# The up/down seam of a hybrid decoder block's MLP: loads placed ahead of a reload, a rectified block moved, additions that free banks placed ahead of sums and low parts

## The chip, the cores and the metric

One core of a Trainium2 chip runs the whole program. The metric is the device time of one launch in microseconds; the kernel before was timed in three runs, and one more execution was profiled.

## The reference

The reference is one decoder layer on a sequence of 1024 tokens of width 1024: two attention mixers, a gate and an output projection, and then the MLP that this case is about, in float32:

```
h = _rms_norm(x, norm_mlp_g[l])
x = x + jnp.square(jax.nn.relu(h @ w_up[l])) @ w_down[l]
return _rms_norm(x, norm_final_g)
```

`w_up` is 1024 x 4096 and `w_down` 4096 x 1024.

## The kernel before, in words

Both products of the MLP are cut into blocks `n`, 16 for `w_up` (n = 0 to 15; `UP` is 16) and 32 for `w_down` (n = 16 to 47). A block is a 2 x 2 product of halves, made with seven products `P1, P2, P6, P5, P7, P4, P3` and some additions of weight blocks and of hidden blocks instead of eight products. Each operand is split into a high part (a cast, made by ScalarE) and a low part (the remainder, made by VectorE), and three products high x high, high x low, low x high stand for one. One product of an up block is 12 matmuls on 128 x 512, one of a down block is 6.

Every engine runs a list that is written out by hand, and semaphores tie the lists together. Around the seam these names count:

- TensorE: `block_products(n)` gives the order. Block 16 of the list is (16,P1) (15,P7) (14,P3) (16,P6) (15,P4) (16,P2) (16,P5) (15,P3); block 17 is (17,P1) (16,P7) (17,P6) (16,P4) (17,P2) (17,P5) (16,P3); from 18 on it is (n,P1) (n-1,P7) (n-1,P3) (n,P6) (n-1,P4) (n,P2) (n,P5). So (18,P4) is the fifth product of block 19.
- The products add up in PSUM banks that are shared between neighbouring blocks. `copy_s1(n)` (L1986) and `copy_s2(n)` (L1998) on ScalarE copy a bank where the next products add on. `dn_add(n, what)` (L2398, `keep<-keep,ps`) on VectorE adds a finished quarter "11", "12", "21" or "22" of a down block to its place in the eight tiles `kp` of 128 x 1024, and so frees its bank: (n,P4) waits for `dn_add(n, "22")`, (n+2,P1) waits for `dn_add(n, "21")`, `copy_s1(n+1)` for `dn_add(n, "11")` and `copy_s2(n+1)` for `dn_add(n, "12")`.
- The tiles of `kp` hold hidden blocks while the up product runs. Before a `dn_add` of blocks 16 to 19 can add to a tile, the residual has to be brought back: `reload(m)` (L885, `keep<-x_mid`, 512 KB) on SyncE's queue. Blocks 16, 17, 18 and 19 use tiles (0,2), (1,3), (4,6) and (5,7), quarters "11" and "12" the first and "21" and "22" the second.
- `load_form(c, j)` (L857, `dn_raw<-hidden`, 512 KB) loads form `j` of the hidden blocks for group `c` of four down blocks. `dn_hi(c, j)` (L2026) and `dn_lo(c, j)` (L2398, `dn_b<-dn_raw,dn_b`) make its high and low parts. Group 0 serves blocks 16 to 19, group 1 blocks 20 to 23.
- `load_a(u, what)` (L841, 256 KB each) loads four blocks of weights for two down blocks. `sums(u)` (L2398, `a_raw` and `spare`) makes their four sums; `form_hi` (L1976) and `form_lo` (L2567) split them.
- `up_c12(q)`, `up_r12(q)` (L2716), `square_12(q)` finish a quarter of up block q; `t_sums(q)` (L2398, `keep<-keep` x4) makes four sums of its quarters, and `store_t(q)` writes them to memory.

All transfers of this stretch are issued by SyncE, in the order of its list, where a transfer stands behind the waits of those ahead of it. Of the waits in that list one counts below:

```
load_unit(UP + 2)
for j in (P2, P5, P7, P4, P3):
    load_form(1, j)
sp.wait_ge(t_ok, 4 * UP - 1)
sp.wait_ge(u11_out[1], 16 * (UP // 2))
reload(4)
```

`t_ok` reaches that count when the third addition of `t_sums(15)` is done.

Of the kernel before, what the change touches and what calls it, by code (L numbers as in the profile page):

```python
# [134 lines left out]
def last_use(u, j):  # L135

    return PRODUCT[u if u < UP else 2 * u - UP + 1, j]
# [27 lines left out]

def dn_forms(n):

    early = {UP + 2: [(1, P6), (1, P2)], UP + 3: [(1, P5), (1, P7)], UP + 4: [(1, P4), (1, P3)]}
    if n in early:
        return early[n]  # L170
    c, pos = divmod(n - UP, 4)
    c += 1 if pos else 0
    if c < 2 or c > 7:
        return []
    return [(c, j) for j in ((P3,), (P1, P6, P2), (P5,), (P7, P4))[pos]]
# [120 lines left out]
def build(nc, x, g_attn, w_in, b_forget, w_branch, w_out, g_mlp, w_up, w_down, g_final, rope, f_rows, r_rows, m_rows, a_rows, x_mid, hidden, sg, out):  # L296
# [8 lines left out]
    with ExitStack() as ctx:  # L305
# [416 lines left out]
        def _(sp):  # L722
# [120 lines left out]
            def load_form(c, j):  # L843

                if c >= 2:
                    sp.wait_ge(done, PRODUCT[UP + 4 * c - 5, j])
                    sp.wait_ge(b_hi, D_FORM[c - 1, j])
                else:
                    sp.wait_ge(done, PRODUCT[UP - 1, P7 if j == P5 else j])
                    if c == 1:  # L850
                        sp.wait_ge(b_hi, D_FORM[0, j])
                if j in (P1, P3):
                    for i in range(2):
                        sp.wait_ge((u11_out if j == P1 else u22_out)[i], 16 * (c + 1))
                else:
                    sp.wait_ge({P2: u21_out, P6: t2_out, P5: t1_out, P7: t3_out, P4: t4_out}[j], 16 * (2 * c + 2))
                sp.dma_start(dn_raw[j][:, c % 2, 1, :, :],  # L857
                             hidden[2 * c:2 * c + 2, j].rearrange("k p c -> p k c")).then_inc(tile_in[j], 16)
# [23 lines left out]
            def reload(m):  # L882
                for i in range(2):
                    sp.wait_ge(x_out[i], 64)
                sp.dma_start(kp[:, m, :], x_mid[m]).then_inc(x_back[m], 16)  # L885
# [138 lines left out]
            sp.wait_ge(u22_out[0], 16 * (UP // 2))  # L1024
            reload(1)
            load_form(0, P3)
            sp.wait_ge(r12_ok, UP)
            reload(3)

            def load_unit(u):  # L1030
                sp.wait_ge(a_lo, A_FORM[u - 2, 2])
                load_a(u, "a21")
                load_a(u, "a22")
                if u == UP + 2:
                    load_form(1, P1)
                    load_form(1, P6)
                sp.wait_ge(done, last_use(u - 2, P1))
                load_a(u, "a11")
                sp.wait_ge(done, last_use(u - 2, P2))
                load_a(u, "a12")  # L1040
# [541 lines left out]
        def _(act):  # L1582
# [382 lines left out]
            def form_hi(q, b):  # L1965

                if b == 0:
                    act.wait_ge(a_in[q % 4], 64 * (q // 4 + 1 + (NG // 2 if q % 4 < 2 else 0)))
                else:
                    act.wait_ge(a_sum, 4 * NG + 4 * q + (0, 3, 4)[b])  # L1970
                if q >= 2:
                    act.wait_ge(done, last_use(q - 2, (P2, P5, P3)[b]))
                elif q == 1:
                    act.wait_ge(w_used, CH_OUT + (KC - 1 if b == 0 else KC))
                src = third_raw(q) if b == 2 else a_raw_t[q % 2][b]
                act.copy(a_hi_t[q % 2][b][:], src[:]).then_inc(a_hi, 1)  # L1976

            def copy_s1(q):
                act.wait_ge(done, PRODUCT[q, P1])
                if q < 2:  # L1980
                    act.wait_ge(hf_lo, H_FORM["t13", 0])
                elif q <= UP:
                    act.wait_ge(r11_ok, q - 1)
                else:
                    act.wait_ge(c11_ok, q - UP + 2)
                act.copy(s1[q] if q < 2 else bank_b(q), bank_a(q)).then_inc(s1_ok, 1)  # L1986
# [13 lines left out]
            def copy_s3(q):  # L2000
                act.wait_ge(done, PRODUCT[q, P7])
                if q == 0:
                    act.wait_ge(hf_lo, H_FORM["t13", 2])
                else:
                    act.wait_ge(c22_ok, NG + q)
                act.copy(s3, bank_a(q)).then_inc(s3_ok, 1)
# [5 lines left out]
            def square_22(q):  # L2012
                square_hidden(u22[q % 2], r22_ok, q + 1, u22_ok)

            def square_12(q):
                square_hidden(u12, r12_ok, q + 1, u12_ok)
# [7 lines left out]
            def dn_hi(c, j):  # L2024
                act.wait_ge(tile_in[j], 16 * (c + 2))
                act.copy(dn_b[j][:, c % 2, 0, :, :], dn_raw[j][:, c % 2, 1, :, :]).then_inc(b_hi, 1)  # L2026
# [60 lines left out]
                square_11(n)  # L2087
            copy_s1(UP)
            copy_s3(UP - 1)
            square_22(UP - 1)  # L2090
            square_12(UP - 2)
            dn_hi(0, P2)
            form_hi(UP, 2)
            dn_hi(0, P5)
            copy_s2(UP)
            dn_hi(0, P7)
            square_21(UP - 1)
            dn_hi(0, P4)
            copy_s1(UP + 1)
            square_12(UP - 1)  # L2100
            form_hi(UP + 1, 0)
            dn_hi(0, P3)
            form_hi(UP + 1, 1)
            dn_hi(1, P1)
            copy_s2(UP + 1)
            form_hi(UP + 1, 2)

# [43 lines left out]
        def _(dve):  # L2151
# [541 lines left out]
            def up_r22(q):  # L2693
                dve.wait_ge(c22_ok, NG + q + 1)
                dve.scalar_tensor_tensor(out=u22[q % 2], in0=u22[q % 2], scalar=0.0, in1=rstd_r,
                                         op0=ALU.max, op1=ALU.mult).then_inc(r22_ok, 1)
# [11 lines left out]
            def up_c12(q):  # L2708
                dve.wait_ge(done, PRODUCT[q, P3])
                dve.wait_ge(s2_ok, NG + q + 1)  # L2710
                after(dve, t1_out, 16 * q)
                add(u12, bank_c(q), s2[q % 2]).then_inc(c12_ok, 1)
# [89 lines left out]
            dn_lo(0, P6)  # L2802
            up_c22(UP - 1)
            up_r22(UP - 1)
            up_c12(UP - 2)
            up_r12(UP - 2)
            dn_lo(0, P2)
            t_sums(UP - 2, (1, 2))
            dn_lo(0, P5)
            form_lo(UP, 2)  # L2810
            t_sums(UP - 2, (3, 4))
            up_r21(UP - 1)
            dn_lo(0, P7)
            dn_add(UP, "11")
            sums(UP + 1)
            up_c12(UP - 1)
            up_r12(UP - 1)
            dn_lo(0, P4)
            dn_add(UP, "22")
            form_lo(UP + 1, 0)  # L2820
            dn_add(UP, "21")
            dn_lo(0, P3)
            dn_add(UP + 1, "11")
            form_lo(UP + 1, 1)
            dn_add(UP, "12")
            t_sums(UP - 1)
            dn_lo(1, P1)
            dn_add(UP + 1, "22")
            for n in range(UP + 2, NB + 1):
                forms = dn_forms(n)  # L2830
                u = form_of(n) + 1
                more = u < N_FORM and n > UP + 1
                if n >= NB:
                    ends = final_events(n - 1)
                    dn_add(n - 1, "22")
                    dn_last(n - 1, "22")
                    for i in ends[:2]:
                        final_sum(i)
                    dn_add(n - 1, "12")
                    dn_last(n - 1, "12")  # L2840
                    for i in ends[2:]:
                        final_sum(i)
                    dn_add(n - 1, "21")
                elif n % 2 == 0:
                    form_lo(u - 1, 2)
                    if more:
                        sums(u, (1,))
                    if n > UP + 2:
                        dn_add(n - 1, "22")
                    if more:  # L2850
                        sums(u, (2,))
                    dn_add(n - 1, "12")
                    if more:
                        sums(u, (3, 4))
                    dn_add(n - 1, "21")
                    for x in forms:
                        dn_lo(*x)
                    dn_add(n, "11")
                else:
                    for x in forms[:2]:  # L2860
                        dn_lo(*x)
                    dn_add(n - 1, "22")
                    if more:
                        form_lo(u, 0)
                    dn_add(n - 1, "12")
                    if more:
                        form_lo(u, 1)
                    dn_add(n - 1, "21")
                    for x in forms[2:]:
                        dn_lo(*x)  # L2870
                    dn_add(n, "11")
                if NB > n > NB - 4:
                    dn_last(n - 1, "22")
                    dn_last(n - 1, "12")
                for i in final_events(n) if n != NB - 1 else ():
                    final_sum(i)
# [61 lines left out]
```

## Time and profile before

| | |
|---|---|
| median of 3 runs | 1521.97 us (1521.58 to 1523.61) |
| profiled execution | 1520.79 us, of which the span is 1519.0 us |
| TensorE busy | 1489.0 us, 98% of the span |
| VectorE busy | 1089.4 us, 72% |
| ScalarE busy | 793.7 us, 52% |
| granted TensorE clock, mean | 0.997 |

The span runs from the first to the last instruction of the program. The up product begins at about 874 us of it, the first down product at 1172.9 us, and the last down product ends at about 1496 us. A busy share is an average over the whole program; the seam is a stretch of some 50 us of it.

### The profile page before, as it was taken

How to read it: one execution, taken by the hardware profiler on the slowest of the kernel's cores; microseconds unless marked ns; L12 is line 12 of the kernel's file. 1: busy time of each engine (PE TensorE's matmuls, PEld its weight loads, DVE VectorE, ACT ScalarE, POOL GpSimd, SP SyncE). 2: the span in 40 equal slices, each digit the busy share in tenths (PEclk: the TensorE clock that was granted, in tenths of full speed). 3: DMA queues.
4: the chain of work that ended last, by engine and by line, in shares of the span. 5: the costliest groups of instructions: out<-in, count | busy, mean ns of one | idle time of the engine just before them, and what ended most of it. 6: DMA issues, size and time to landing. Idle time of an engine off the chain costs nothing.

```text
span 1519.0 us, 20720 instructions
## 1 busy us (share of the span) xinstructions
PE 1489.0 (98%) x7283; PEld 1235.1 (81%) x7283; DVE 1089.4 (72%) x1745; ACT 793.7 (52%) x1440; POOL 18.6 (1%) x29
## 2 busy tenths in 40 slices
PE   7999999999999999999999999999999899999997
PEld 6888888887888888888888888888888688888886
DVE  5787777756786778543765686667667898888876
ACT  6577766665677775444234553333434544444432
POOL 0000000000000200000000000000000000000001
PEclk9999999999999999999999999999999999999998
DMA  5221111114222014334545434444445964444402
GB/s 194 71 70 29 43 56 43 29 45 101 70 70 71 15 43 127 96 104 149 180 135 140 139 104 164 154 153 152 152 153 178 313 214 152 152 153 152 153 28 111
DMA packets 171061, 176.78 MB, mean 116 GB/s; under 512 B 9576, under 2 KB 129736, under 8 KB 170576
## 3 DMA queue, kind: packets, MB, share of 16 engines
q1 hardware_dynamic: 170960, 175.46, 36.3%
q8 instruction: 60, 0.98, 0.3%
q14 instruction: 41, 0.34, 0.1%
HBM read 129.08 MB, written 46.35 MB: 115 GB/s over the span
## 4 chain that ended last, share of the span: by engine, by line
PE 87%; DVE 6%; ACT 2%; issue 2%; DMA 2%; SPq 1%; DVEq 0%; ACTq 0%
PE ps L1545 37%; PE ps L1204 20%; PE ps L1405 8%; PE ps L1149 4%; PE ps L1436 4%; PE ps L1280 3%; PE ps L1247 3%; PE ps L1259 3%; PE ps L1346 1%; DVE keep L2398 1%; PE ps L1138 1%; PE ps L1173 1%; DVE keep L2293 1%; DVE ps L2271 1%; PE ps L1293 0%
## 5 line engine op out<-in xcount | busy, mean ns | idle before, releaser
L1204 PE MATMUL ps<-hspl,wsp 128*128 128x512 f32 x1536 | 419.5, 407 | 0.4 <-ACT tmp L1634 0.4
L1204 PEld LDWEIGHTS ps<-hspl,wsp 128*128 128x128 f32 x1536 | 265.8, 189 | 43.5 <-ACT tmp L1634 0.6
L1545 PE MATMUL ps<-dn_b,a_hi 128*128 128x512 f32 x896 | 276.4, 390 | 5.7 <-DVE keep L2398 3.5
L1545 PEld LDWEIGHTS ps<-dn_b,a_hi 128*128 128x128 f32 x896 | 167.6, 188 | 43.0 <-issue 7.4
L1545 PE MATMUL ps<-dn_b,a_lo 128*128 128x512 f32 x448 | 174.3, 389 | 0.0
L2398 DVE TENSOR_TENSOR keep<-keep,ps 128x512 f32<-128x512 f32 (+1 forms) x144 | 102.1, 714 | 60.0 <-PE ps L1545 41.0
L1545 PE MATMUL ps<-up_b,a_hi 128*128 128x512 f32 x384 | 118.5, 390 | 0.2 <-DVE up_b L2398 0.2
L2010 ACT ACTIVATE keep<-keep 128x512 f32<-128x512 f32 x64 | 40.5, 633 | 126.6 <-DVE keep L2705 42.0
L1545 PEld LDWEIGHTS ps<-dn_b,a_lo 128*128 128x128 f32 x448 | 84.1, 188 | 17.5
L2567 DVE TENSOR_TENSOR a_lo<-a_raw,a_hi 128x1024 fp32r<-128x1024 f32 (+1 forms) x66 | 81.3, 1234 | 9.5 <-ACT a_hi L1976 9.3
L2293 DVE TENSOR_TENSOR keep<-ps,o_part 64x256 f32<-64x256 f32 x80 | 39.8, 497 | 62.7 <-ACT o_part L1725 61.3
L1545 PEld LDWEIGHTS ps<-up_b,a_hi 128*128 128x128 f32 x384 | 71.9, 188 | 15.6 <-DVE up_b L2398 0.7
L1986 ACT COPY ps<-ps 128x512 f32<-128x512 f32 x46 | 26.3, 571 | 111.4 <-PE ps L1545 109.1
L1545 PE MATMUL ps<-up_t,a_hi 128*128 128x512 f32 x256 | 79.1, 390 | 0.1
L1545 PE MATMUL ps<-up_t4b,a_hi 128*128 128x512 f32 x256 | 78.8, 389 | 0.0
L1710 ACT CAST work<-ps 128x128 fp32r<-128x128 f32 (+3 forms) x144 | 50.8, 365 | 51.1 <-PE ps L1259 50.1
L1259 PE MATMUL ps<-ident,tmp 128*128 128x128 f32 x428 | 73.4, 274 | 2.7 <-ACT tmp L1702 2.4
L1545 PE MATMUL ps<-up_b,a_lo 128*128 128x512 f32 x192 | 74.7, 389 | 0.0
L1280 PEld LDWEIGHTS ps<-work 128*128 128x128 f32 x456 | 68.3, 190 | 6.0 <-issue 0.2
L1259 PEld LDWEIGHTS ps<-ident,tmp 128*128 128x128 f32 x428 | 53.7, 140 | 22.7 <-ACT tmp L1702 8.5
L2398 DVE TENSOR_TENSOR dn_b<-dn_raw,dn_b 128x1024 fp32r<-128x1024 f32 x56 | 67.0, 1219 | 3.9 <-ACT dn_b L2026 3.9
L1976 ACT CAST a_hi<-a_raw 128x1024 fp32r<-128x1024 f32 (+1 forms) x66 | 68.3, 1060 | 2.3 <-DMA a_raw<-in_w_up 2.2
(227 smaller groups left out, 2804.5 us busy)
## 6 DMA issues: line engine op xcount, KB each, us to landing
hidden<-keep SPq DMA_DIRECT2D x112, 256.0 KB, 2.2
dn_raw<-hidden SPq DMA_DIRECT2D x56, 512.0 KB, 6.1
raw<-in_w_in SPq DMA_DIRECT2D x35, 512.0 KB, 3.8
a_raw<-in_w_up SPq DMA_DIRECT2D x36, 256.0 KB, 3.1
sgl<-sg SPq DMA_DIRECT2D x8, 1024.0 KB, 5.0
a_raw<-in_w_down SPq DMA_DIRECT2D x32, 256.0 KB, 3.0
spare<-in_w_down SPq DMA_DIRECT2D x32, 256.0 KB, 3.7
spare<-in_w_up SPq DMA_DIRECT2D x28, 256.0 KB, 3.1
```

What stands on the lines that cost most here:

```text
L1149: ins = pe.matmul(ps[:, cols], w(wp, k), mv(mp, k)[:, cols], start=(k == 0 and n == 0), stop=(k == ks - 1 and n == 2))
L1204: ins = pe.matmul(psp(u, g), wsp[c % 2][:, wp, k * P:(k + 1) * P], hspl[:, mp, k, cols], start=(n == 0), stop=(n == 23), skip_group_check= ...
L1259: ins = pe.transpose(o[:, (k - a) * P:(k - a + 1) * P], probs(G)[:, k * P:(k + 1) * P], ident[:])
L1280: ins = pe.matmul(o[:, cols], v_nat[:, j, 2 * (b % 2):2 * (b % 2) + 2, :].rearrange("p a d -> p (a d)"), moving, start=(part == 0 and (n = ...
L1405: ins = pe.matmul(o, (a_hi_t, a_lo_t)[wp][q % 2][b][:, i, k * P:(k + 1) * P], gate_b(j, mp, k), start=(j in (P1, P5) and k == 0 and m == 0 ...
L1436: ins = pe.matmul(banks[a][:, cols], w_of(c)(wp, k), br_in[:, mp, k, cols], start=(k == ks[0] and n == 0), stop=(k == ks[-1] and n == 2), ...
L1545: ins = pe.matmul(o, a_part(n, j, wp, k), b_block(n, j, mp, k), start=(first and k == 0 and m == 0), stop=(k == ks - 1 and m == 2), skip_g ...
L1710: act.copy(pt_tiles(G, 0, a, b), tr_bank(G, u)[:, 0:(b - a) * P].rearrange("p (j c) -> p j c", c=P)).then_inc(pt_hi, 1)
L1976: act.copy(a_hi_t[q % 2][b][:], src[:]).then_inc(a_hi, 1)
L2293: dve.tensor_tensor(pair_tokens(dst[row:row + 64], t, b // 2), pair_view(o_bank(B)[row:row + 64, :], t), pair_view(o_part[row:row + 64, :] ...
L2398: return dve.tensor_tensor(out, a, b, op)
L2567: dve.tensor_tensor(a_lo_t[q % 2][b][:], src[:], a_hi_t[q % 2][b][:].bitcast(F32), ALU.subtract).then_inc(a_lo, 1)
```

## The change

SyncE's list: `load_form(1, P1)`, the first two weight blocks of unit 18 and `load_form(1, P6)` are issued ahead of the wait for `up_r12(15)` and of `reload(3)`, which stood in front of them. ScalarE's list: `dn_hi(0, ...)` of P2, P5 and P3 each stand ahead of a square or a cast; `square_12(15)` stands behind both casts of unit 17; `dn_hi(1, P1)` moves from in front of `copy_s2(17)` to block 18. VectorE's list: `dn_lo(0, P2)` stands ahead of `up_c12(14)`; `dn_add(16, "22")` ahead of `sums(17)`; `dn_add(16, "12")` and `dn_add(17, "22")` each move ahead; `dn_lo(1, P1)` moves to block 18, and there all sums and low parts stand behind the three additions. TensorE's list does not change.

```
 def dn_forms(n):
-    early = {UP + 2: [(1, P6), (1, P2)], UP + 3: [(1, P5), (1, P7)], UP + 4: [(1, P4), (1, P3)]}
+    early = {UP + 2: [(1, P1), (1, P6), (1, P2)], UP + 3: [(1, P5), (1, P7)], UP + 4: [(1, P4), (1, P3)]}
...
             load_form(0, P3)
-            sp.wait_ge(r12_ok, UP)
-            reload(3)
+            load_form(1, P1)
             def load_unit(u):
                 sp.wait_ge(a_lo, A_FORM[u - 2, 2])
                 load_a(u, "a21")
                 load_a(u, "a22")
                 if u == UP + 2:
-                    load_form(1, P1)
                     load_form(1, P6)
+                    sp.wait_ge(r12_ok, UP)
+                    reload(3)
...
             copy_s3(UP - 1)
+            dn_hi(0, P2)
             square_22(UP - 1)
+            form_hi(UP, 2)
             square_12(UP - 2)
-            dn_hi(0, P2)
-            form_hi(UP, 2)
             dn_hi(0, P5)
...
             copy_s1(UP + 1)
+            dn_hi(0, P3)
+            form_hi(UP + 1, 0)
+            form_hi(UP + 1, 1)
             square_12(UP - 1)
-            form_hi(UP + 1, 0)
-            dn_hi(0, P3)
-            form_hi(UP + 1, 1)
-            dn_hi(1, P1)
             copy_s2(UP + 1)
             form_hi(UP + 1, 2)
...
+            dn_lo(0, P2)
             up_c12(UP - 2)
             up_r12(UP - 2)
-            dn_lo(0, P2)
-            t_sums(UP - 2, (1, 2))
+            t_sums(UP - 2, (1,))
             dn_lo(0, P5)
+            t_sums(UP - 2, (2,))
             form_lo(UP, 2)
             t_sums(UP - 2, (3, 4))
             up_r21(UP - 1)
             dn_lo(0, P7)
             dn_add(UP, "11")
+            dn_lo(0, P4)
+            dn_add(UP, "22")
             sums(UP + 1)
             up_c12(UP - 1)
             up_r12(UP - 1)
-            dn_lo(0, P4)
-            dn_add(UP, "22")
+            dn_lo(0, P3)
+            dn_add(UP, "21")
             form_lo(UP + 1, 0)
-            dn_add(UP, "21")
-            dn_lo(0, P3)
+            dn_add(UP, "12")
             dn_add(UP + 1, "11")
             form_lo(UP + 1, 1)
-            dn_add(UP, "12")
+            dn_add(UP + 1, "22")
             t_sums(UP - 1)
-            dn_lo(1, P1)
-            dn_add(UP + 1, "22")
             for n in range(UP + 2, NB + 1):
...
+                elif n == UP + 2:
+                    form_lo(u - 1, 2)
+                    dn_add(n - 1, "12")
+                    dn_add(n - 1, "21")
+                    dn_add(n, "11")
+                    sums(u)
+                    for x in forms:
+                        dn_lo(*x)
```

In SyncE's list, between the reload of tile 1 and the third weight block of unit 18, the two lists differ as follows (`keep<-x_mid` is a reload: the first row that of tile 1, the moved one that of tile 3; `dn_raw_103`, `97` and `99` are forms P3 of group 0 and P1 and P6 of group 1):

```order
 L885 DMA keep<-x_mid 128x1024
 L857 DMA dn_raw_103<-hidden 128x2x512
-L885 DMA keep<-x_mid 128x1024
-L841 DMA spare_88<-in_w_down 128x2x256 x2
-L857 DMA dn_raw_97<-hidden 128x2x512
-L857 DMA dn_raw_99<-hidden 128x2x512
+L857 DMA dn_raw_97<-hidden 128x2x512
+L841 DMA spare_88<-in_w_down 128x2x256 x2
+L857 DMA dn_raw_99<-hidden 128x2x512
+L885 DMA keep<-x_mid 128x1024
 L841 DMA a_raw_0_82<-in_w_down 128x2x256 x2
 L857 DMA dn_raw_98<-hidden 128x2x512
```

The reload of tile 3 goes behind two forms and two weight blocks. The reload of tile 4, which comes after five more forms, keeps its place.

In VectorE's list of before, this stands from the two sums after `form_lo(17, 2)` to `dn_add(18, "22")` (`keep_51<-keep_51,ps` is a `dn_add`: "12" and "21" of block 17, "11" and "22" of block 18; `a_raw0` and `spare0` are `sums(18)`; `dn_b2`, `1`, `3`, `4` are the low parts of forms P6, P2, P5, P7 of group 1):

```order
L2398 TENSOR_TENSOR spare0_88<-a_raw0_0_82,spare0_88 128x512
L2398 TENSOR_TENSOR keep_51<-keep_51,ps3 128x512
L2398 TENSOR_TENSOR a_raw0_1_83<-a_raw0_1_83,a_raw0_0_82 128x512
L2398 TENSOR_TENSOR spare0_88<-a_raw0_0_82,a_raw0_1_83 128x512
L2398 TENSOR_TENSOR keep_51<-keep_51,ps0 128x512
L2398 TENSOR_TENSOR dn_b2_92<-dn_raw2_99,dn_b2_92 128x1024
L2398 TENSOR_TENSOR dn_b1_91<-dn_raw1_98,dn_b1_91 128x1024
L2398 TENSOR_TENSOR keep_51<-keep_51,ps3 128x512
L2398 TENSOR_TENSOR dn_b3_93<-dn_raw3_100,dn_b3_93 128x1024
L2398 TENSOR_TENSOR dn_b4_94<-dn_raw4_101,dn_b4_94 128x1024
L2398 TENSOR_TENSOR keep_51<-keep_51,ps0 128x512
```

In VectorE's list of the changed kernel, the same stretch from `dn_add(17, "21")` on reads (lines are one less there; `dn_b0` is form P1):

```order
L2397 TENSOR_TENSOR keep_51<-keep_51,ps0 128x512
L2397 TENSOR_TENSOR keep_51<-keep_51,ps3 128x512
L2397 TENSOR_TENSOR a_raw0_1_83<-spare0_88 128x512
L2397 TENSOR_TENSOR spare0_88<-a_raw0_0_82,spare0_88 128x512
L2397 TENSOR_TENSOR a_raw0_1_83<-a_raw0_1_83,a_raw0_0_82 128x512
L2397 TENSOR_TENSOR spare0_88<-a_raw0_0_82,a_raw0_1_83 128x512
L2397 TENSOR_TENSOR dn_b0_90<-dn_raw0_97,dn_b0_90 128x1024
L2397 TENSOR_TENSOR dn_b2_92<-dn_raw2_99,dn_b2_92 128x1024
L2397 TENSOR_TENSOR dn_b1_91<-dn_raw1_98,dn_b1_91 128x1024
L2397 TENSOR_TENSOR dn_b3_93<-dn_raw3_100,dn_b3_93 128x1024
L2397 TENSOR_TENSOR dn_b4_94<-dn_raw4_101,dn_b4_94 128x1024
L2397 TENSOR_TENSOR keep_51<-keep_51,ps0 128x512
```

`dn_add(18, "11")`, the second row, moved from behind two low parts to the front of `sums(18)`; between it and `dn_add(18, "22")`, the last row, there are now four sums and five low parts, where there were two low parts.

## Rows read from the trace of the kernel before

**Rows 1.** Windows: start:end, length, PE, PEld, DVE, ACT, POOL busy, PEclk, DMA, GB/s.

```profile
1190.00:1200.00 10.00, 7.25 (x33) 5.69 (x32) 9.22 (x13) 5.61 (x7) 0.00 (x0) 1.00 0.81 263
1200.00:1210.00 10.00, 9.10 (x41) 7.23 (x40) 9.33 (x12) 5.35 (x6) 0.00 (x0) 1.00 1.04 372
1210.00:1220.00 10.00, 9.93 (x44) 7.78 (x42) 9.93 (x13) 4.96 (x6) 0.00 (x0) 1.00 0.87 315
```

**Rows 2.** TensorE's waits from 1100 to 1496: total us, times, longest.

```profile
PE ps L1545 <- DVE keep L2398: 3.5, 2, 2.8
PE ps L1545 <- issue: 1.3, 2, 0.9
PE ps L1545 <- ACT ps L1998: 0.9, 1, 0.9
```

**Rows 3.** TensorE's timeline at the seam: start, us, instruction, idle before and releaser.

```profile
1184.28 0.70 PE L1545 MATMUL ps<-dn_b,a_hi 128*128 128x512 f32 x2 [0.35 <-issue]
...
1186.84 0.69 PE L1545 MATMUL ps<-dn_b,a_hi 128*128 128x512 f32 x2 [0.94 <-issue]
...
1198.04 0.70 PE L1545 MATMUL ps<-dn_b,a_hi 128*128 128x512 f32 x2 [2.75 <-DVE keep L2398]
...
1202.23 0.61 PE L1545 MATMUL ps<-dn_b,a_hi 128*128 128x512 f32 x2
...
1203.60 0.61 PE L1545 MATMUL ps<-dn_b,a_hi 128*128 128x512 f32 x2
...
1206.02 0.70 PE L1545 MATMUL ps<-dn_b,a_hi 128*128 128x512 f32 x2 [0.90 <-ACT ps L1998]
...
1220.25 0.70 PE L1545 MATMUL ps<-dn_b,a_hi 128*128 128x512 f32 x2
```

**Rows 4.** VectorE's timeline, from the low part of (0, P2) on.

```profile
1182.95 1.23 DVE L2398 TENSOR_TENSOR dn_b<-dn_raw,dn_b 128x1024 fp32r<-128x1024 f32 x1 [1.64 <-ACT dn_b L2026]
...
1204.40 2.71 DVE L2398 TENSOR_TENSOR keep<-keep 128x512 f32<-128x512 f32 x4
...
1208.77 1.75 DVE L2567 TENSOR_TENSOR a_lo<-spare,a_hi 128x1536 fp32r<-128x1536 f32 x1
1210.43 0.68 DVE L2398 TENSOR_TENSOR a_raw<-spare 128x512 f32<-128x512 f32 x1
...
1214.28 2.35 DVE L2398 TENSOR_TENSOR dn_b<-dn_raw,dn_b 128x1024 fp32r<-128x1024 f32 x2
...
1217.15 2.35 DVE L2398 TENSOR_TENSOR dn_b<-dn_raw,dn_b 128x1024 fp32r<-128x1024 f32 x2
1219.42 0.68 DVE L2398 TENSOR_TENSOR keep<-keep,ps 128x512 f32<-128x512 f32 x1
```

**Rows 5.** SyncE's queue: issues of the reloads of tiles 1 and 4.

```profile
1191.62 0.32 SPq L885 DMA_DIRECT2D keep<-x_mid  x1
...
1206.54 0.33 SPq L885 DMA_DIRECT2D keep<-x_mid  x1
```

**Rows 6.** Issue to landing, us: form P2 at 1173.38, reloads at 1191.62, 1196.18, 1206.54, 1215.72.

```profile
dn_raw<-hidden SPq DMA_DIRECT2D x1, 512.0 KB, 5.4
...
keep<-x_mid SPq DMA_DIRECT2D x1, 512.0 KB, 4.0
...
keep<-x_mid SPq DMA_DIRECT2D x1, 512.0 KB, 3.5
...
keep<-x_mid SPq DMA_DIRECT2D x1, 512.0 KB, 8.5
...
keep<-x_mid SPq DMA_DIRECT2D x1, 512.0 KB, 3.4
```

**Rows 7.** ScalarE's timeline: the high part of (1, P1), ahead of `copy_s2(17)`.

```profile
1204.34 1.05 ACT L2026 CAST dn_b<-dn_raw 128x1024 fp32r<-128x1024 f32 x1 [4.69 <-DMA dn_raw<-hidden]
```

**Rows 8.** Windows of the program's tail, columns as in Rows 1.

```profile
1500.00:1505.00 5.00, 3.56 (x27) 3.24 (x28) 4.14 (x7) 0.69 (x2) 0.00 (x0) 0.86 0.00 0
1505.00:1510.00 5.00, 5.00 (x26) 5.00 (x25) 3.30 (x5) 1.44 (x3) 2.36 (x1) 0.50 0.52 210
```

## The prediction

> **What bounds the kernel now.** I read the totals first: TensorE is busy for 98% of the span, so only a stretch where it waits can give time back. The list of its waits from the last up products to the last down product shows that there is little: 5.7 us in all [rows 2]. The timeline puts 4.9 us of it at the seam, in front of (16,P2) at 1184.28, (16,P5) at 1186.84, (16,P4) at 1198.04 and (17,P7) at 1206.02 [rows 3]. The reader should then look at who is late there. The windows show VectorE busy for 9.22, 9.33 and 9.93 us of three stretches of ten, and a DMA share of 0.81 to 1.04 [rows 1]. So from about 1183 to 1220 the seam is bound by VectorE's list, fed by a full queue. At 1220.25 TensorE starts (18,P4), 0.15 us after the end of `dn_add(18, "22")`, which began at 1219.42 and took 0.68 [rows 3, 4]. That is the point which fixes the end: behind it TensorE runs through. Whatever the change wins earlier counts only if `dn_add(18, "22")` comes earlier too, so the whole sum is the shift of that one instruction, plus what a longer wait there costs.
>
> **The change, seam first.** The low part of (0,P2) now goes ahead of `up_c12(14)`. Its form was issued at 1173.38 and took 5.4 us to land [rows 6], so it is there at 1178.8; the cast takes 1.05 (that of another form [rows 7]), and the low part starts at 1179.9 instead of 1182.95 [rows 4]. (16,P2) no longer waits. `dn_add(16, "22")` stands before `sums(17)` and comes about 4 us earlier, which takes away the 2.75 us in front of (16,P4) [rows 3]. `copy_s2(17)` loses its place behind the cast of (1,P1), which had kept ScalarE waiting 4.69 us for a transfer [rows 7]; that takes away most of the 0.90 at (17,P7) [rows 3]. Working down the three lists with the durations of these rows I get (17,P7) at about 1202, 4 us earlier than before, with 1.5 us of short waits left (for the low parts of (0,P5) and (0,P3)). The edits on ScalarE cost nothing of their own: it is busy 5 to 6 us of ten [rows 1].
>
> **The change, VectorE.** Before `t_sums(15)` the list now holds all it held after the low part of (0,P2), that is 1204.40 - 1182.95 = 21.45 us, less idle time of about 1.4 us (0.78 and 0.67 in the first two windows [rows 1]), plus `up_c12(14)` and `up_r12(14)` (1.3 us) and `dn_add(17, "22")` (0.60). From 1179.9 that ends at 1202 if nothing waits. I find about 2 us of waits (for `square_12(14)`, the form of (0,P5), and the end of (17,P7) near 1203.3, for which `dn_add(17, "22")` must wait), so `t_sums(15)` starts near 1204.1, against 1204.40 [rows 4]: nearly where it was.
>
> From there to `dn_add(18, "22")` the work is: `t_sums` 2.63, `form_lo(17, 2)` 1.66, three `dn_add` at 0.60, `sums(18)` 2.65 (1210.43 to 1214.28 holds it and two `dn_add`), five low parts at 1.14 (2.27 for two). The sum is 2.63 + 1.66 + 1.80 + 2.65 + 5.70 = 14.4 us [rows 4]. From 1204.1 it ends at 1218.5, 0.9 us earlier than 1219.42. That is all the list can gain if nothing waits in it.
>
> **The change, the new wait.** `dn_add(18, "11")` adds to tile 4 and needs its reload. Before, it stood behind two low parts and began at 1216.6, after the reload had landed: issued at 1206.54, 8.5 us, so 1215.0 [rows 5, 6]. Now it stands ahead of `sums(18)` and is reached at 1204.1 + 2.63 + 1.66 + 1.2 = 1209.6. Queued behind it are the four sums and five low parts, 8.35 us, and then `dn_add(18, "22")`, for which TensorE waits.
>
> When does the reload land now? It can't be issued before the third addition of `t_sums(15)`, 2.14 us after their start as before, so at 1206.2, and in front of it in the queue stands what stood there before: from the reload of tile 1 on, 13 pieces of 512 KB. At 372 to 400 GB/s (the second window shows 372 [rows 1]) a piece takes 1.3 to 1.4 us. Two things make the queue earlier. The reload of tile 1 follows the stores of up block 15, which I find 0.6 us earlier. And the old order had a hole: the reload of tile 1 landed at 1195.6, that of tile 3 at 1199.7 [rows 5, 6], 4.1 us with just one other piece between, where two pieces take 2.7; the loads that were put ahead fill these 1.4 us. So it lands at 1215.0 - 0.6 - 1.4 = 1213.0. Bounds: if the queue were empty, the fastest reload took 3.4 us [rows 6], which gives 1209.6, just when VectorE comes; if the queue gains nothing it stays at 1215.0. I take 1213.0, since the windows show the DMA engines full and the rows that it comes from are of this very queue.
>
> Then `dn_add(18, "22")` starts at 1213.0 + 0.60 + 2.65 + 5.70 = 1222.0 (0.60 is `dn_add(18, "11")` itself), 2.6 us later than 1219.42. With the bounds it is 1218.6 (0.8 us earlier) to 1224.0 (4.6 later). **First term: +2.6 us.**
>
> TensorE, ahead by now, does ten products from (17,P7) at 1202, of 1.37 us each (1202.23 to 1203.60 [rows 3]), and stands before (18,P4) from about 1215.6. All the small waits of the seam are gathered there in one of about 7 us, more than twice the longest so far, 2.75 [rows 3]. That may lower the clock. In the seam of before the granted clock stayed at 1.00 through that 2.75 us [rows 1]. In the tail it fell: 0.86 and 0.50 of full speed in two windows, where TensorE had waited and done little [rows 8]; 0.50 is the 1.2 GHz level. About 1.4 + 5.0 us went by at that level. If TensorE worked at half speed for 5.4 us it would lose 2.7; if the clock stays it loses nothing. I take 1.8, nearer the upper end, since a stand of 7 us is longer than the one in the tail, but less than all of it because the tail's work was short pieces. Behind (18,P4) no wait is left in which such a loss could hide. **Second term: +1.8 us.**
>
> The Trainium skill (TensorE: Matmul & The Clock Gate, section on HAM oscillation) says that a group of matmuls that comes after a long enough wait starts at the half clock, and that this is paid each time. By it the second term stands; by the seam's row alone, where 1.00 was kept, the sum would be 2.6. The tail agrees with the rule; no wait of 7 us among large matmuls is in this trace.
>
> **Sum.** +2.6 + 1.8 = +4.4 us. The profiled execution took 1520.79 (1519.0 and 1.8 around it), the median is 1521.97; I put the shift on the median: **1526.4 us**.
>
> **The rivals.**
> - The reload and VectorE as above, but the clock stays: +2.6, 1524.6 (from +0.8 to +3.3). For it: 1.00 in every window of the seam [rows 1].
> - The reload lands by the time VectorE is there. Then the pile behind it starts at 1209.6, and `dn_add(18, "22")` comes 0.8 us earlier: 1521.2, not slower. The point that decides: it must land before 1210.4. Against it: 512 KB pieces fill the queue until then, and none of them was taken out.
> - The seam's waits are won in full, -5.7 us, 1516.3. Then `dn_add(18, "22")` would have to start near 1214; VectorE's work alone, without any wait, ends it at 1216.4 (1202 + 14.4). That allows -3.0 at most, so this needs a mistake in my account of what (18,P4) waits for.
> - More than forecast, over +6: forms land later as five large loads compete earlier (form P3 of group 0 or the reload of tile 3 late for `dn_add(17, "22")`), and both terms sit at their upper ends: 1528 and more.
>
> **How the numbers follow.** Forecast (wait and lower clock, +3 to +6) 0.52; clock stays 0.20; reload early 0.16; full gain 0.06; more 0.06. A measurement of this kernel can tell about 0.2%, 3.0 us, from no change. Slower by more: 0.51 of the forecast, the last case, and a little of the second: 0.58. Faster by more: 0.06. Within: 0.36. The range leaves out the full gain, the last case and the lower half of the early reload: 1521.5 to 1528.0. The forecast's own is 1524.9 to 1528.0.
>
> **What would show it.** Right: TensorE's waits of 2.75 and 0.90 are gone, (17,P7) starts 3 to 4 us earlier; VectorE idles 2 to 4 us before `dn_add(18, "11")` with the transfer `keep<-x_mid` as releaser; one TensorE wait of 5 to 8 us before (18,P4), released by `dn_add`; a granted clock under 1.00 in the ten us behind it. Wrong: VectorE does not idle there, or (18,P4) starts before 1219, or the clock reads 1.00 throughout.

## The result and the profile after

The changed kernel takes 1525.94 us (median of 11 runs, 1524.50 to 1527.88), the kernel before, run beside it, 1522.14 us (11 runs, 1520.83 to 1523.61). The ratio is 1.0025, with a 95% interval of 1.0016 to 1.0033: about 3.8 us slower. The forecast was 1526.4 us.

TensorE's waits from 1100 to 1500 us of the changed kernel (total us, times, longest), to be held against [rows 2]:

```profile
PE ps L1545 <- DVE keep L2397: 6.9, 2, 6.2
PE ps L1545 <- issue: 1.6, 2, 1.1
```

In sum the waits grew: 8.5 us stand where 5.7 stood. Most of it is one wait of 6.2 us. The timeline of TensorE in the changed kernel shows where it lies (start, us, instruction, idle before and releaser; the rows answer to [rows 3]):

```profile
1185.63 0.70 PE L1545 MATMUL ps<-dn_b,a_hi 128*128 128x512 f32 x2 [1.13 <-issue]
...
1198.89 0.70 PE L1545 MATMUL ps<-dn_b,a_hi 128*128 128x512 f32 x2 [0.51 <-issue]
...
1202.07 0.68 PE L1545 MATMUL ps<-dn_b,a_hi 128*128 128x512 f32 x2
...
1222.12 1.19 PE L1545 MATMUL ps<-dn_b,a_hi 128*128 128x512 f32 x2 [6.18 <-DVE keep L2397]
...
1223.53 1.05 PE L1545 MATMUL ps<-dn_b,a_hi 128*128 128x512 f32 x2
...
1224.81 1.05 PE L1545 MATMUL ps<-dn_b,a_hi 128*128 128x512 f32 x2
...
1226.09 0.79 PE L1545 MATMUL ps<-dn_b,a_hi 128*128 128x512 f32 x2
...
1226.96 0.62 PE L1545 MATMUL ps<-dn_b,a_hi 128*128 128x512 f32 x2
```

The first two are short waits, in front of (16,P5) and (16,P3); those before (16,P2) and (16,P4) are gone, and (17,P7) starts at 1202.07, with none ahead of it. Then (18,P4) at 1222.12 stands behind 6.18 us. The last five rows are read for their distances: three matmuls (one row of two and one of one) took 1.41, 1.28, 1.28 and 0.87 us, 4.84 together, where four such groups take 2.74 in [rows 3] (1202.23 to 1203.60, 1.37, is two of them). The windows say why (columns as in [rows 1]; the eighth number is the granted clock):

```profile
1210.00:1215.00 5.00, 5.00 (x24) 4.14 (x23) 2.58 (x4) 3.40 (x4) 0.00 (x0) 1.00 0.84 316
1215.00:1220.00 5.00, 0.93 (x5) 0.43 (x3) 5.00 (x5) 1.05 (x1) 0.00 (x0) 0.96 0.93 317
1220.00:1225.00 5.00, 2.88 (x7) 2.33 (x8) 4.84 (x6) 1.21 (x2) 0.00 (x0) 0.50 0.26 91
1225.00:1230.00 5.00, 5.00 (x21) 4.01 (x20) 3.04 (x3) 0.84 (x2) 0.00 (x0) 0.86 0.36 80
```

From 1220 to 1225 the clock was 0.50, the 1.2 GHz level; in the window ahead of it TensorE had been busy for 0.93 us of five. VectorE, third pair of the row, idled for half of the first window. Its timeline, which answers to [rows 4], shows for what:

```profile
1204.32 2.71 DVE L2397 TENSOR_TENSOR keep<-keep 128x512 f32<-128x512 f32 x4
1206.94 1.75 DVE L2566 TENSOR_TENSOR a_lo<-spare,a_hi 128x1536 fp32r<-128x1536 f32 x1
1208.62 1.28 DVE L2397 TENSOR_TENSOR keep<-keep,ps 128x512 f32<-128x512 f32 x2
1212.35 0.69 DVE L2397 TENSOR_TENSOR keep<-keep,ps 128x512 f32<-128x512 f32 x1 [2.46 <-DMA keep<-x_mid]
1212.96 0.68 DVE L2397 TENSOR_TENSOR a_raw<-spare 128x512 f32<-128x512 f32 x1
...
1215.61 5.76 DVE L2397 TENSOR_TENSOR dn_b<-dn_raw,dn_b 128x1024 fp32r<-128x1024 f32 x5
1221.29 0.68 DVE L2397 TENSOR_TENSOR keep<-keep,ps 128x512 f32<-128x512 f32 x1
```

`dn_add(18, "11")` at 1212.35 waited 2.46 us for the reload of its tile. The four sums and five low parts went behind it, and `dn_add(18, "22")`, which frees the bank of (18,P4), began at 1221.29. The chain that ended last (start, us, work) goes through just these: the transfer, the pile behind it, TensorE.

```profile
1206.45 5.81 DMA keep<-x_mid
...
1216.75 4.62 DVE dn_b L2397 x4
...
1222.12 7.98 PE ps L1545 x25
```

Two cautions for all comparisons below. The first down product starts at other times in each profile (1172.89 in the kernel before, 1172.10 in this one; 1173.15 in e1, 1175.11 in e2, 1172.77 in e3, 1175.68 in e4, 1173.74 in e5, 1172.75 in e6 and 1173.56 in e10), for reasons ahead of the seam. So I compare distances from it. `dn_add(18, "22")` begins 46.53 us behind it in the kernel before and 49.19 now: 2.66 later. And the kernel before was timed again beside each group of experiments, with medians of 1522.63 us (e1 to e4), 1522.45 (e5 to e7) and 1522.58 (e8, e10) against 1522.14 beside the change. So differences of two medians from different groups are good to about 0.5 us; the ratios are free of this.

### The profile page after: what moved, and what is told of

Its sections match the earlier page's. It is cut to its first block, busy times and chain, and to the rows that moved or that the text cites. A ratio compares the mean times of both kernels' runs of the same rounds, so it can differ in the third digit from the quotient of the medians.

```text
span 1522.7 us, 20720 instructions
## 1 busy us (share of the span) xinstructions
PE 1489.4 (98%) x7283; PEld 1235.2 (81%) x7283; DVE 1088.5 (71%) x1745; ACT 793.9 (52%) x1440; POOL 18.6 (1%) x29
## 4 chain that ended last, share of the span: by engine, by line
PE 87%; DVE 6%; issue 2%; ACT 2%; DMA 2%; SPq 0%; DVEq 0%; ACTq 0%
PE ps L1545 38%; PE ps L1204 20%; PE ps L1405 8%; PE ps L1149 4%; PE ps L1436 4%; PE ps L1280 3%; PE ps L1247 3%; PE ps L1259 3%; PE ps L1346 1%; DVE keep L2397 1%; PE ps L1138 1%; PE ps L1173 1%; DVE keep L2292 1%; DVE ps L2270 1%; PE ps L1293 0%
```

## The experiments

The theory: the move of `dn_add(18, "11")` ahead of the sums makes VectorE wait for a reload with 8.35 us of other work queued behind it, and the long wait of TensorE that follows costs clock on top. The main rival: the two forms and two weight blocks, now issued ahead of the reload of tile 3, crowd the queue, and all transfers of the seam come later. The table has the times and the ratio to the kernel before; each run's edit follows.

| what ran | median us | ratio, 95% interval |
|---|---|---|
| the change | 1525.94 | 1.0025 [1.0016, 1.0033] |
| e1: the change, block 18 as before | 1521.22 | 0.9990 [0.9982, 0.9999] |
| e2: the change, loads as before | 1529.14 | 1.0043 [1.0030, 1.0056] |
| e3: before, with block 18's new order alone | 1527.37 | 1.0031 [1.0020, 1.0043] |
| e4: the change, TensorE's wait filled | 1524.24 | 1.0012 [1.0003, 1.0021] |
| e10: the change, sums ahead of the addition | 1523.61 | 1.0004 [0.9995, 1.0013] |
| e5: low parts behind the additions | 1520.26 | 0.9981 [0.9971, 0.9991] |
| e6: e5, reloads ahead of forms | 1520.98 | 0.9985 [0.9976, 0.9994] |
| e7: old seam, e6's blocks and reloads | 1522.11 | 0.9997 [0.9988, 1.0006] |
| e8: e6, an addition ahead in block 20 | 1520.21 | 0.9985 [0.9977, 0.9994] |

**e1: VectorE's order in block 18 undone.** All other edits of the change stay.

```diff
-                elif n == UP + 2:
-                    form_lo(u - 1, 2)
-                    dn_add(n - 1, "12")
-                    dn_add(n - 1, "21")
-                    dn_add(n, "11")
-                    sums(u)
-                    for x in forms:
-                        dn_lo(*x)
```

> The changed kernel with VectorE's list of block 18 put back (sums between the additions, low parts ahead of dn_add(18, 11)); low part of (1,P1) stays in block 18. Theory (the reload of tile 4 is waited for with sums and low parts queued behind it): no idle time of VectorE for a reload, dn_add(18, 22) about 2.5 us earlier than in the changed kernel, the wait before (18,P4) 3 to 4 us instead of 6.2, and less or no time at the lower clock: 1521.0 to 1522.0, ratio 0.999 to 1.000. Rival (the loads put ahead of the reload, or the edits at the seam, cost the time): about 1526, as the changed kernel.

It took 1521.22 us, and the loss is gone. The loads were still issued early, so they are not what costs the time: the rival falls. `dn_add(18, "22")` comes at 1219.26, 46.11 us behind the first down product. In this kernel TensorE's one wait of note with two later rows (the last is (18,P4)), VectorE's addition, and two windows read:

```profile
1213.21 0.71 PE L1545 MATMUL ps<-dn_b,a_hi 128*128 128x512 f32 x2 [2.23 <-DVE keep L2397]
...
1217.59 0.67 PE L1545 MATMUL ps<-dn_b,a_hi 128*128 128x512 f32 x2
...
1220.36 0.62 PE L1545 MATMUL ps<-dn_b,a_hi 128*128 128x512 f32 x2
```

```profile
1219.26 0.68 DVE L2397 TENSOR_TENSOR keep<-keep,ps 128x512 f32<-128x512 f32 x1
```

```profile
1210.00:1215.00 5.00, 2.77 (x11) 1.97 (x10) 4.96 (x7) 2.48 (x3) 0.00 (x0) 0.93 0.91 347
1215.00:1220.00 5.00, 5.00 (x18) 4.02 (x17) 5.00 (x7) 2.49 (x3) 0.00 (x0) 0.73 0.86 295
```

The old order makes TensorE wait for `dn_add(17, "21")` before (19,P1) instead, and the clock fell here too. That costs little: TensorE started (18,P4) at 1220.36, 0.42 us behind the end of the addition (1219.94), where 0.15 was the distance in the kernel before. Of the 1.6 us that the clock took, all but about 0.3 would have been waited there.

**e2: SyncE's edit undone.** The reload of tile 3 and its wait go back ahead of the loads of (1,P1) and (1,P6).

```diff
-            load_form(1, P1)
+            sp.wait_ge(r12_ok, UP)
+            reload(3)
...
                 if u == UP + 2:
+                    load_form(1, P1)
                     load_form(1, P6)
-                    sp.wait_ge(r12_ok, UP)
-                    reload(3)
```

> The changed kernel with SyncE's list put back: the reload of tile 3 ahead of the form (1,P1), two weight blocks and the form (1,P6). Theory: the hole in the queue is back, the reload of tile 4 lands 1 to 2 us later, and all of that is on the path: 1527 to 1528, ratio 1.003 to 1.004. Rival (the loads ahead of the reload crowd the queue and cause the loss): 1522 to 1524.

It took 1529.14 us, slower than the change. So the early loads help, which is against the rival a second time, and by more than I expected: `dn_add(18, "11")` begins 43.07 us behind the first down product where it was 40.25 in the change, 2.8 later, and the time is above the expected band. VectorE's row of `dn_add(18, "11")` shows the longer wait for the reload, and TensorE has two waits of its own:

```profile
1218.18 0.69 DVE L2397 TENSOR_TENSOR keep<-keep,ps 128x512 f32<-128x512 f32 x1 [6.23 <-DMA keep<-x_mid]
```

```profile
1219.67 1.19 PE L1545 MATMUL ps<-dn_b,a_hi 128*128 128x512 f32 x2 [3.06 <-ACT ps L1986]
...
1227.94 1.20 PE L1545 MATMUL ps<-dn_b,a_hi 128*128 128x512 f32 x2 [5.37 <-DVE keep L2397]
```

The first stands behind `copy_s1`, which needs the bank that `dn_add(18, "11")` frees. I had not counted it. Both rows last 1.19 to 1.20 us, where such a row lasts 0.70 at full clock: the clock fell twice.

**e3: the new order of block 18 alone, in the kernel before.** The branch shown at e1 is put in, nothing else.

> The kernel before with VectorE's order of block 18 alone: three additions, then the sums, then the low parts. Theory: dn_add(18, 11) waits for the reload until about 1215, then four sums and four low parts, 7.2 us, so dn_add(18, 22) starts near 1222.8 instead of 1219.4, and the wait before (18,P4) is 3 to 4 us: 1525 to 1526, ratio 1.002 to 1.0026, with 2 us more if the clock falls. Rival (the loss needs the new place of the loads or the earlier TensorE): 1522.

It took 1527.37 us: this one move by itself is at least as slow as the whole change. VectorE and TensorE:

```profile
1215.15 0.69 DVE L2398 TENSOR_TENSOR keep<-keep,ps 128x512 f32<-128x512 f32 x1 [3.28 <-DMA keep<-x_mid]
...
1222.96 0.68 DVE L2398 TENSOR_TENSOR keep<-keep,ps 128x512 f32<-128x512 f32 x1
```

```profile
1223.78 1.19 PE L1545 MATMUL ps<-dn_b,a_hi 128*128 128x512 f32 x2 [4.47 <-DVE keep L2398]
```

VectorE waits for the same reload (3.28 us here) with the same pile behind it; the first matmul row lasts 1.19 us, so the clock fell after 4.47 us as well. By the medians the rest of the change wins 1.4 us back, by the ratios 0.9; the two intervals overlap, so this gain is not shown.

**e4: TensorE's wait filled.** In the changed kernel, 24 matmuls that add nothing to the output run while TensorE would wait for (18,P4), into a bank that a later product, (19,P5), overwrites.

```diff
+                    if (q, j) == (UP + 2, P4):
+                        pe.wait_ge(c12_ok, NG + UP)
+                        for i in range(24):
+                            pe.matmul(bank_c(UP + 3), a_part(UP + 3, P6, 0, 0),
+                                      b_block(UP + 3, P6, 0, 0), start=True, stop=True, ...)
```

> The changed kernel with 24 matmuls more on TensorE ahead of (18,P4), 5.4 us of work, into a bank that a later product clears; they do nothing for the output. Theory (the second term is the clock): the granted clock stays at 1.00 from 1215 to 1230, matmuls behind (18,P4) take their usual 0.68 us for three, dn_add(18, 22) does not move: 1.5 to 2.5 us less than the changed kernel, 1523.5 to 1524.5, ratio 1.001 to 1.0016. Rival (the slow stretch comes from the wait's end itself and not from the idle time): no gain, 1526 or more.

It took 1524.24 us, 1.7 less than the change, with more work in it. TensorE's timeline (the first row is at (16,P3)), VectorE's addition and the windows:

```profile
1203.41 0.70 PE L1545 MATMUL ps<-dn_b,a_hi 128*128 128x512 f32 x2 [2.28 <-issue]
...
1220.31 5.61 PE L1554 MATMUL ps<-dn_b,a_hi 128*128 128x512 f32 x24
1225.75 0.62 PE L1545 MATMUL ps<-dn_b,a_hi 128*128 128x512 f32 x2
```

```profile
1224.82 0.68 DVE L2402 TENSOR_TENSOR keep<-keep,ps 128x512 f32<-128x512 f32 x1
```

```profile
1200.00:1205.00 5.00, 2.72 (x11) 1.64 (x10) 3.32 (x4) 3.48 (x4) 0.00 (x0) 1.00 1.07 384
1205.00:1210.00 5.00, 4.94 (x22) 3.90 (x22) 4.08 (x7) 4.15 (x5) 0.00 (x0) 1.00 1.05 382
...
1220.00:1225.00 5.00, 5.00 (x24) 4.14 (x23) 5.00 (x6) 0.00 (x0) 0.00 (x0) 1.00 0.92 307
1225.00:1230.00 5.00, 5.00 (x24) 4.06 (x23) 5.00 (x7) 1.97 (x2) 0.00 (x0) 1.00 0.06 20
```

The clock stays at 1.00, and the addition stays where it was in the change (49.14 us behind the first down product, 49.19 there; everything in this profile lies 3.6 us later, since its first down product does). This separates the two terms: the clock is worth 1.7 us by the medians of e4 and the change, 2.2 with each against the kernel before that ran beside it, and what is left, 1.6 to 2.1 us, is the late addition. The two intervals just overlap; that the clock costs time is shown by the matmul rows as well, its size to about half a microsecond.

**e10: the sums go into the wait.** One line of the changed kernel moves; the low parts stay behind the addition.

```diff
-                    dn_add(n, "11")
                     sums(u)
+                    dn_add(n, "11")
```

> The changed kernel with one move: sums(18) ahead of dn_add(18, 11), the low parts stay behind it. Theory: the reload lands as before, the four sums (2.65 us) lie in the wait for it (2.46 us), so dn_add(18, 22) starts 2.4 us earlier, near 1218.9 on the changed kernel's clock, and the wait before (18,P4) is 3.7 us: 1523 to 1523.7 if the clock still falls, ratio 1.0006, and 1521.5 if it stays. Rival (what is lost depends on the low parts alone or on the transfer alone): no change, 1526.

It took 1523.61 us, 2.3 less than the change, and its interval takes in no difference from the kernel before. `sums(18)` needs no reload, so VectorE does it while the transfer is under way; `dn_add(18, "11")`, the first row below, then starts without a wait. The rows of VectorE and TensorE:

```profile
1213.26 0.68 DVE L2397 TENSOR_TENSOR keep<-keep,ps 128x512 f32<-128x512 f32 x1
1213.85 5.76 DVE L2397 TENSOR_TENSOR dn_b<-dn_raw,dn_b 128x1024 fp32r<-128x1024 f32 x5
1219.53 0.68 DVE L2397 TENSOR_TENSOR keep<-keep,ps 128x512 f32<-128x512 f32 x1
```

```profile
1220.36 1.19 PE L1545 MATMUL ps<-dn_b,a_hi 128*128 128x512 f32 x2 [3.66 <-DVE keep L2397]
```

The addition is 45.97 us behind the first down product, 3.2 earlier than in the change. The clock falls after 3.66 us too: the row lasts 1.19.

**e5: the low parts behind the additions.** As e10, and three of the five low parts move behind `dn_add(18, "22")`. Block 19 gets a list of its own.

```diff
-    early = {UP + 2: [(1, P1), (1, P6), (1, P2)], UP + 3: [(1, P5), (1, P7)], UP + 4: [(1, P4), (1, P3)]}
+    early = {UP + 2: [(1, P1), (1, P6)], UP + 3: [(1, P2), (1, P5)], UP + 4: [(1, P7), (1, P4), (1, P3)]}
...
-                    dn_add(n, "11")
                     sums(u)
+                    dn_add(n, "11")
+                    for x in forms:
+                        dn_lo(*x)
+                elif n == UP + 3:
+                    dn_add(n - 1, "22")
+                    form_lo(u, 0)
+                    dn_add(n - 1, "12")
+                    form_lo(u, 1)
+                    dn_add(n - 1, "21")
                     for x in forms:
                         dn_lo(*x)
+                    dn_add(n, "11")
```

> The changed kernel with sums(18) ahead of dn_add(18, 11) and the low parts of group 1 not needed yet (P2, P5, P7) behind dn_add(18, 22) and its two neighbours; casts follow. Theory: the reload of tile 4 lands as in the changed kernel, two low parts stand between it and dn_add(18, 22), which then waits only for the reload of tile 6 and starts about 5 us earlier; the wait before (18,P4) shrinks from 6.2 to 1 to 2 us and the clock stays: 1518.5 to 1519.5, ratio 0.998. Rival (VectorE's total work bounds this stretch however it is ordered): 1521, as with the block 18 order of before.

It took 1520.26 us, ratio 0.9981, faster than both kernels. The ratio is as expected, the time 0.8 us above its band. VectorE's addition, TensorE's product behind it, and the window:

```profile
1216.97 0.69 DVE L2397 TENSOR_TENSOR keep<-keep,ps 128x512 f32<-128x512 f32 x1 [1.09 <-DMA keep<-x_mid]
```

```profile
1217.80 0.70 PE L1545 MATMUL ps<-dn_b,a_hi 128*128 128x512 f32 x2 [1.41 <-DVE keep L2397]
```

```profile
1215.00:1220.00 5.00, 3.60 (x17) 2.66 (x16) 3.91 (x5) 1.70 (x4) 0.00 (x0) 1.00 0.94 306
```

`dn_add(18, "22")` now waits only for the reload of its own tile, 43.23 us behind the first down product, 3.30 earlier than in the kernel before; the clock stays at 1.00.

**e6: e5 with the reloads ahead of forms.** SyncE issues the forms P7, P4 and P3 of group 1 behind reloads 6, 5 and 7, so that the reload that e5 waits for lands sooner.

```diff
-            for j in (P2, P5, P7, P4, P3):
+            for j in (P2, P5):
                 load_form(1, j)
...
             reload(6)
+            load_form(1, P7)
...
             reload(5)
+            load_form(1, P4)
...
             reload(7)
+            load_form(1, P3)
```

> As e5, and on SyncE the reloads of tiles 4, 6, 5, 7 ahead of the forms P7, P4, P3 of group 1. Theory: the reload of tile 4 has no more than two forms before it and lands 2 to 3 us earlier than in the changed kernel, that of tile 6 too; no wait over 1 us is left before (18,P4): 1517 to 1518, ratio 0.9970. Rival (the forms that come later are now waited for in blocks 20 and 21, and take the gain): 1519 to 1522 with waits of TensorE behind 1225.

It took 1520.98 us: nothing won over e5, and the theory missed. The rows at (18,P4) and in block 20:

```profile
1216.20 0.69 DVE L2400 TENSOR_TENSOR keep<-keep,ps 128x512 f32<-128x512 f32 x1 [0.27 <-DMA keep<-x_mid]
```

```profile
1217.03 0.70 PE L1548 MATMUL ps<-dn_b,a_hi 128*128 128x512 f32 x2 [0.58 <-DVE keep L2400]
```

```profile
1226.32 0.69 DVE L2400 TENSOR_TENSOR a_raw<-spare 128x512 f32<-128x512 f32 x1 [1.43 <-DMA a_raw<-in_w_down]
```

```profile
1227.75 0.70 PE L1548 MATMUL ps<-dn_b,a_hi 128*128 128x512 f32 x2 [0.95 <-DVE keep L2400]
```

VectorE's wait for the reload of tile 6 shrank from 1.09 to 0.27 us, but `dn_add(18, "22")` came no earlier: 43.45 us behind the first down product, against 43.23 in e5. So there was no gain at (18,P4) to give back. Behind it a new wait shows, as the rival said, though for weights and not for forms: the third row is VectorE at the sums of block 20, waiting for weight blocks, the last TensorE, waiting for the addition that stands behind them.

**e7: the old seam with e6's later blocks.** The kernel before, with e6's lists for blocks 18 and 19, its order of forms and its reloads.

> The kernel before, its seam as it was, with the order of blocks 18 and 19 and the order of the reloads of e6 alone. Theory: TensorE's waits of 2.75 and 0.9 us at the seam stay, nothing is gained behind them since (18,P4) hardly waited: 1521.5 to 1522.5, ratio 1.000; the edits at the seam and those behind it pay only together. Rival (the order of blocks 18 and 19 wins by itself): 1518 to 1519.

It took 1522.11 us, no change. The seam's wait stays, in TensorE's row

```profile
1201.63 0.70 PE L1548 MATMUL ps<-dn_b,a_hi 128*128 128x512 f32 x2 [2.75 <-DVE keep L2401]
```

So the later blocks alone (e7) bring nothing that can be told, and the other edits of the change alone (e1) 0.1%; together (e6) it is 0.15%, where the intervals of e1 and e6 overlap.

**e8: an addition ahead in block 20.** As e6, with `dn_add(19, "22")` ahead of the sums that wait for weights.

```diff
+                    if n == UP + 4:
+                        dn_add(n - 1, "22")
                     if more:
                         sums(u, (1,))
-                    if n > UP + 2:
+                    if n > UP + 4:
                         dn_add(n - 1, "22")
```

> As e6, and in block 20 dn_add(19, 22) ahead of the first of sums(19), behind which it stood while that waited for weight blocks that now land later (VectorE idle 1.43 us, TensorE 0.95 us before (19,P4) in e6). Theory (e6 gave its gain back there): that wait of TensorE is gone, 0.5 to 1 us less than e6: 1519.5 to 1520.5, ratio 0.998. Rival (the difference between e5 and e6 is form P3 of group 0 landing later, or scatter): as e6, 1521.

It took 1520.21 us. The wait of 0.95 us is gone from the trace, but the ratio is that of e6. The 0.8 us between the medians lie within both intervals, so the run settles nothing about the time.

## Why the prediction was right

- **The place that fixes the end.** It was `dn_add(18, "22")` and (18,P4), as said. Undoing only what delays it (e1) removes the loss, doing only that in the kernel before (e3) brings it.
- **The seam.** (17,P7) was put at 1202 and started at 1202.07, the waits left were put at 1.5 us and are 1.64 (1.13 + 0.51). Counted from the first down product, the gain is 3.2 us and not 4, since this profile runs 0.79 ahead.
- **The first term, +2.6.** Measured from the first down product it is +2.66. Its parts were less exact than their sum. On the clock of the kernel before (0.79 added), `t_sums(15)` began at 1205.1 (1204.1 predicted), VectorE reached `dn_add(18, "11")` at 1210.7 (1209.6), and the reload was issued at 1207.2 (1206.2). All three are a microsecond late. The transfer took 5.8 us where 6.8 was worked out, and so it landed at 1213.0, as predicted. The wait was 2.46 and not 3.4, but only the landing counts for what follows. That the landing came out so exactly is luck: of the 2.0 us by which it was put earlier, 0.6 was for the reload of tile 1, which was issued (row below) 18.91 us behind the first down product, 0.18 later than before [rows 5]. The loads put ahead gave more than the 1.4 allowed for them; without them (e2) `dn_add(18, "11")` begins 2.8 us later. The two errors cancelled. (The reload of tile 4 has twelve such pieces in front of it by the list, not 13; no sum uses the count.)

```profile
1191.01 0.32 SPq L885 DMA_DIRECT2D keep<-x_mid  x1
```

- **The second term, +1.8.** The four slow groups of matmuls cost 4.84 - 2.74 = 2.1 us in the trace of the change, and filling the wait gained 1.7 to 2.2 (e4). That the clock would fall was right: it read 0.50 behind the wait, and the seam's own 1.00 through 2.75 us did not carry over. The size was in part luck. The working from the tail has a slip, 1.4 + 5.0 being 6.4 and not 5.4, so that the upper end would be 3.2; and [rows 8] show TensorE busy for 3.56 and 5.00 us of five there, which is not little. TensorE's longest wait in the tail before the clock fell (row below) was 1.65 us, shorter than the 2.75 that left the clock alone, so the tail did not show that the length of a wait decides. In the change the windows give about 6.8 us at the lower level (0.4, 5.0 and 1.4 of three windows), but it began inside the wait, and TensorE worked for some 4 us of it, which is why the loss is 2.1. The Trainium skill (TensorE: Matmul & The Clock Gate, section on HAM oscillation) says that a group of matmuls behind a long enough wait starts at the half clock; this trace agrees, with 1.19 us for the first row of two behind 6.18 us, where 0.70 is usual.

```profile
1497.88 3.09 PE L1574 MATMUL ps<-ident,keep 128*128 128x128 f32 x24 [1.65 <-DVE keep L2398]
```

- **The sum.** Both terms of the trace give 4.8; from the first to the last down product the profiled executions differ by 4.7 (322.7 and 327.4). The medians differ by 3.8, and the two profiled executions as a whole by 3.7 (1524.52 and 1520.79): the earlier start of the first down product, 0.79, makes nearly all of the 0.9 between. Why it started earlier is open; single executions of one kernel scatter by more (1524.50 to 1527.88).
- **The rivals.** The full queue did not clear by 1210.4, so the early landing fell. The clock did not stay. What the account left out is `copy_s1`: e2 shows that a later reload makes a second wait of TensorE through it, so the upper bound of the first term (4.6) was too mild; it did not come to that here. The last rival speaks of five large loads; the change puts four ahead, two forms and two weight blocks.

## What to carry to other kernels

When an instruction of an in-order list waits for a transfer, count what is queued behind it, and put ahead of it what needs no transfer: the four sums alone gave 2.3 us back by the medians (e10), with low parts moved as well the kernel became faster than before (e5). Removing several short waits ahead of a fixed point gathers them into one, and for TensorE one long wait can cost more than the short ones did, where the clock falls behind it (1.7 to 2.2 us in e4). So move the point itself, the addition that frees the bank, before winning time in front of it.

## What the runs showed of the hardware

- The length of a wait alone did not decide whether the clock fell. It fell behind waits of 6.18 (the change), 4.47 (e3), 3.66 (e10) and 2.23 us (e1: 0.73 in the window from 1215 to 1220), but stayed at 1.00 through 2.75 us in the kernel before [rows 1, 3] and, in e4, through a wait of 2.28 us in front of (16,P3), at 1203.41. What else decides is not settled by these runs.
- Work that adds nothing can pay: 24 matmuls in the wait kept the clock at 1.00 and made the kernel 1.7 us faster than the change without them (e4).
- A fall of the clock costs little where TensorE would have waited anyway: e1 lost 1.6 us in four groups of matmuls (1213.21 to 1217.59 is 4.38, against 2.74), of which about 0.3 was left at (18,P4), and was still no slower than the kernel before.
